# Output projection of a hybrid decoder layer: eight block products replaced by seven, for pairs of token tiles

## The reference, cut to what matters

```python
merged = g_m[:, :, 0] * (o_nsa @ w_up_nsa) + g_m[:, :, 1] * (o_dil @ w_up_dil)
mixer = merged @ w_o                                  # (1024 x 1024) @ (1024 x 1024)
x = x + g1 * mixer
h = rmsnorm(x, norm2) * (1 + sc2) + sh2
lg = h @ wg + bg;  grp = argmax(lg)                   # 4 groups of 8 experts
le = (h @ we + be) of that group;  top_v, top_i = top_k(le, 2)
x = x + g2 * (sum over the two experts of weight * (silu(h @ w1[e]) * (h @ w3[e])) @ w2[e])
out = rmsnorm(x, norm_f)
```

## Time and profile before

| | us |
|---|---|
| median of 3 runs | 1779.27 |
| lowest and highest of them | 1778.99, 1780.42 |
| the profiled execution | 1781.83 |
| its span, first to last instruction | 1780.0 |
| mean granted TensorE clock | 0.981 |

### The profile page before, as it was taken

How to read it: one execution, slowest core, us unless ns; L and a number is a source line. 1 busy time by engine, 2 the same in 40 slices (tenths; PEclk the granted TensorE clock), 3 DMA queues, 4 the chain that set the end, 5 groups by cost and what they waited for, 6 DMA issues and landing times. The chain is left out here.

```text
span 1780.0 us, 37158 instructions
## 1 busy us (share of the span) xinstructions
PE 1686.5 (95%) x16053; PEld 1128.6 (63%) x16053; DVE 607.3 (34%) x1569; ACT 415.1 (23%) x933; POOL 177.2 (10%) x219
## 2 busy tenths in 40 slices
PE   5999999999999999999999999999999999998992
PEld 3444445898777777644444445558777777777772
DVE  4533331002667666666555322261111011010103
ACT  4000000002666656510100011122212221211122
POOL 1205000000111010000000000001111111111110
PEclk9999999999999999999999999999999999999996
DMA  9874224221101107334433182149999999999985
GB/s 340 250 225 116 71 79 144 51 85 42 34 11 43 32 2 245 104 102 127 142 120 89 28 329 96 48 179 403 397 392 396 396 398 399 393 389 390 387 308 209
DMA packets 155456, 355.74 MB, mean 200 GB/s; under 512 B 15519, under 2 KB 94999, under 8 KB 138875
## 3 DMA queue, kind: packets, MB, share of 16 engines
q1 hardware_dynamic: 128112, 303.14, 45.6%
q0 software_dynamic: 13456, 27.93, 5.8%
q10 hardware_dynamic: 13724, 22.27, 3.6%
HBM read 321.58 MB, written 47.13 MB: 207 GB/s over the span
## 5 line engine op out<-in xcount | busy, mean ns | idle before, releaser
L2451 PE MATMUL psum<-sb_m_xT,sb_m_ring 128*64 128x64 f32 (+1 forms) x4096 | 174.4, 244 | 6.4 <-issue 4.2
L2451 PEld LDWEIGHTS psum<-sb_m_xT,sb_m_ring 128*64 128x64 f32 x4096 | 167.5, 138 | 19.1 <-issue 17.3
L2347 DVE TENSOR_TENSOR sb_m_hT<-psum,sb_m_sg 128x128 f32<-128x128 f32 (+1 forms) x64 | 22.1, 345 | 349.0 <-ACT sb_m_sg L2226 349.0
L2226 ACT ACTIVATE sb_m_sg<-psum 128x128 f32<-128x128 f32 (+1 forms) x64 | 20.5, 320 | 419.3 <-PE psum L2451 419.3
L2451 PE MATMUL psum<-sb_m_xT,sb_front 128*64 128x64 f32 (+1 forms) x2560 | 108.2, 242 | 9.6 <-DMA sb_m_ring<-in_exp_w_dram 4.9
L2451 PEld LDWEIGHTS psum<-sb_m_xT,sb_front 128*64 128x64 f32 x2560 | 102.7, 139 | 17.8 <-issue 16.7
L1724 PE MATMUL psum<-sb_w_o_sb,sb_mT 128*128 128x512 f32 x256 | 112.9, 595 | 0.0
L728 PE MATMUL psum<-sb_vD,sb_room 128*128 128x512 f32 x240 | 104.7, 593 | 0.2 <-DVE sb_vD L671 0.2
L2213 ACT ACTIVATE sb_m_xT<-psum,sb_rowmod 128x64 f32<-128x64 f32 (+1 forms) x256 | 84.6, 436 | 38.9 <-PE psum L2439 38.9
L988 ACT ACTIVATE sb_d_probs<-sb_d_probs,sb_d_nmax 128x640 f32<-128x640 f32 (+7 forms) x128 | 92.9, 735 | 1.5 <-DVE sb_d_nmax L1028 1.0
L760 PE MATMUL psum<-sb_b_wvd,sb_rows 128*128 128x256 f32 x384 | 88.9, 394 | 0.0
(11 more groups left out here) (346 smaller groups left out, 2418.5 us busy)
## 6 DMA issues: line engine op xcount, KB each, us to landing
sb_m_ring<-in_exp_w_dram SPq DMA_DIRECT2D x48, 2048.0 KB, 30.2
sb_front<-in_exp_w_dram SPq DMA_DIRECT2D x30, 2048.0 KB, 31.6
sb_rows<-in_exp_w_dram SPq DMA_DIRECT2D x18, 2048.0 KB, 31.1
sb_g_ada<-in_ada_w_dram SPq DMA_DIRECT2D x16, 1024.0 KB, 5.2
d_qk<-sb_n_b_sel ACTq DMA_DIRECT2D x20, 512.0 KB, 3.0
sb_front<-in_w_in_dram SPq DMA_DIRECT2D x16, 512.0 KB, 5.2
sb_front<-d_qk SPq DMA_DIRECT2D x15, 512.0 KB, 6.9
sb_n_b_sel<-in_w_in_dram SPq DMA_DIRECT2D x10, 512.0 KB, 8.9
```

What stands on the lines that cost most here:

```text
L2451: mm = pe.matmul(k.psum[part, c // 2, col:col + w], views[which][:, kk, c * P + CAPS * h:c * P + CAPS * (h + 1)], x[:, kk, 0:w], start=(kk ...
```

## The change

The 1024 x 1024 product `merged @ w_o` is cut into 2 x 2 blocks: tokens in tile `u` and tile `u + 4`, input channels in two halves, output channels in two halves. For each pair of tiles `u` (four of them), seven products M1 to M7 of four matmuls each take the place of 32 matmuls. They are computed from sums of blocks:

- sums of the weight blocks, once: `t1 = b12 - b11`, `t2 = b22 - t1` on VectorE, and `b12 <- b22 - b12`, `t4 = t2 - b21` on GpSimd, each 128 x 2048;
- sums of the activations, four of 128 x 512 for each pair, on VectorE (`row_sums`, `row_sum3`, `row_sum4`);
- sums of the products, on VectorE: each of the four result blocks takes one more addition (in `residual`), and three partial sums (`add`: u2, u5, u3); ScalarE copies M1 out of PSUM (`m1`).

The seven products go through four PSUM banks in turn. Tiles are routed in the order `TILE = [4, 0, 5, 1, 6, 2, 7, 3]`, in pairs behind the products of the next pair. `choose` runs for the first four positions while the last pair is computed, and for the other four at the end (`FIRST = NT - 4`), and the last product M3 stands behind the count of the first four. The weight sums `t1`, `t2` live in slot 2 of `front`, so the first expert's third matrix is fetched only after the last product and behind the last store. One of the three idle products at the end of the first stage is taken away, and one is added (four for three) before the last count.

```diff
+TILE = [4, 0, 5, 1, 6, 2, 7, 3]
...
-            idle_products(pe, k, 4, 3)
+            idle_products(pe, k, 4, 2)
...
+        t1, t2 = wide(2 * 4 * D), wide(2 * 4 * D + HK * BANK)
+        t4 = sb("t4", [P, HK, BANK])[:, :, :]
+        bank = lambda u, i: (7 * u + i) % 4
...
-        FIRST = NT - 2
+        FIRST = NT - 4
...
-            for i, w in enumerate((k.exp_w1, k.exp_w3, k.exp_w2)):
+            for i, w in enumerate((k.exp_w1, k.exp_w3)):
...
+            sp.wait_ge(s_done, done(NPAIR - 1, M3))
+            sp.dma_start(*expert_matrix(k.exp_w2, slice(0, 1), k.front[:, 4 * D * 2:4 * D * 3], True)).then_inc(k.s_first[2], 16)
...
+            for u in range(NPAIR):
+                a11, a12, a21, a22 = quarters(u)
+                product(u, M1, a11, b11)
+                if u == 0:
                     pe.wait_ge(s_last, 1)
+                else:
+                    turn(2 * u - 2, 0)
+                    turn(2 * u - 2, 1)
+                product(u, M2, a12, b21)
+                if u >= 1:
...
+                    route(2 * u - 2)
+                    turn(2 * u - 1, 0)
+                    turn(2 * u - 1, 1)
+                pe.wait_ge(s_sums, 4 * u + 2)
+                pe.wait_ge(s_wide, 2)
+                product(u, M6, s2, t2)
+                if u >= 1:
+                    route(2 * u - 1)
+                product(u, M5, s1, t1)
...
+                pe.wait_ge(s_wide2, 1)
+                product(u, M7, a21, b12)
+                pe.wait_ge(s_wide2, 2)
+                product(u, M4, a22, t4)
+                if u == NPAIR - 1:
+                    pe.wait_ge(s_hot, 1)
...
+                    for t in range(FIRST):
+                        mm = later(t, False)
+                    mm.then_inc(s_rank, 1)
+                pe.wait_ge(s_sums, 4 * u + 4)
+                product(u, M3, a12, b22)
+            turn(NT - 2, 0)
+            turn(NT - 2, 1)
             turn(NT - 1, 0)
+            route(NT - 2)
             turn(NT - 1, 1)
             route(NT - 1)
-            pe.wait_ge(s_mul, 2 * NT - 2)
-            idle_products(pe, k, 1, 3)
+            pe.wait_ge(s_used, used(NPAIR - 1, C12))
+            idle_products(pe, k, 1, 4)
...
+            dve.wait_ge(s_wo, 32)
+            tt(t1, b12, b11, ALU.subtract).then_inc(s_wide, 1)
+            dve.wait_ge(s_wide, 1)
+            tt(t2, b22, t1, ALU.subtract).then_inc(s_wide, 1)
+            row_sums(0)
...
+        @block.gpsimd
+        def _(pool):
+            pool.wait_ge(s_wo, 32)
+            pool.wait_ge(s_wide, 1)
+            pool.tensor_tensor(b12, b22, b12, ALU.subtract).then_inc(s_wide2, 1)
+            pool.wait_ge(s_wide, 2)
+            pool.tensor_tensor(t4, t2, b21, ALU.subtract).then_inc(s_wide2, 1)
```

More of the change, by code:

```diff
@@ L1685, in stage_out @@
         s_sum, s_sum0 = k.sem("h_sum"), k.sem("h_sum_first")
+        s_done, s_used, s_m1, s_sums, s_wide, s_wide2 = (k.sem("h_" + n) for n in (
+            "products", "products_used", "m1_out", "row_sums", "column_sums", "column_sums_pool"))
         s_x2 = [k.sem(f"h_residual{i}") for i in range(4)]
@@ L1721, in _, with product @@
         def _(pe):
[L1722 to L1727, removed]
+            def product(u, i, x, w):
+                n = 7 * u + i
+                if n >= 4:
+                    was, j = divmod(n - 4, 7)
+                    pe.wait_ge(s_m1 if j == M1 else s_used, was + 1 if j == M1 else used(was, last_use[j]))
+                for kk in range(HK):
+                    mm = pe.matmul(k.psum[:, bank(u, i), :], x[:, kk, :], w[:, kk, :], start=(kk == 0), stop=(kk == HK - 1))
+                mm.then_inc(s_done, 1)
             ones, tri = k.const[:, K_ONE:K_ONE + P], k.const[:, K_TRI:K_TRI + P]
@@ L1772, in _ @@
                     mm.then_inc(s_shift, 1)
[L1773 to L1790 removed]
+                pe.wait_ge(s_sums, 4 * u + 3)
+                pe.wait_ge(s_wide2, 1)
[4 more added lines that the diff above has]
+                    pe.wait_ge(s_hot, 1)
+                    pe.wait_ge(s_modT, 2)
+                    pe.matmul(k.psum[:, 7, 0:(NT + 1) * NE], tri, both.rearrange("p t e -> p (t e)"), start=True, stop=False)
+                    for t in range(FIRST):
[5 more added lines that the diff above has]
+            turn(NT - 2, 1)
+            turn(NT - 1, 0)
+            route(NT - 2)
             turn(NT - 1, 1)
[L1792 to L1794 removed]
             route(NT - 1)
[L1796 to L1797 removed]
+            pe.wait_ge(s_used, used(NPAIR - 1, C12))
+            idle_products(pe, k, 1, 4)
             pe.wait_ge(s_hot, 2)
@@ L1892, in _ @@
             v.inc(dve.memset(both[:, FIRST:, :], 0.0)); v.wait(dve)
-            for t in range(NT):
-                if t == NT - 1:
-                    dve.wait_ge(s_sum0, 16)
-                    dve.wait_ge(s_xn, 1)
-                    choose(0, FIRST)
-                residual(t, 0)
-                if t >= 1:
-                    turned(t - 1)
-                    if t == 1:
+            row_sum3(0)
+            for u in range(NPAIR + 1):
+                if u >= 1:
+                    root(2 * u - 2)
+                    if u == 1:
                         dve.wait_ge(s_shift, 1)
```

202 lines of the change are left out of this document (131 added, 71 removed).

## The result

The changed kernel takes **1795.15 us** (median of 4 runs, 1793.21 to 1796.25) beside 1779.57 us for the kernel before (4 runs on the same chip): a ratio of **1.0086**, 95% interval 1.0069 to 1.0103. It is slower, as forecast, but by 15.6 us instead of 8.9, and 1.2 us above the upper end of the range.

What follows compares the result with a forecast made beforehand. TensorE was taken to be busy nearly everywhere, with DMA full too in the expert stage, which starts from be_i. Terms -2.8 + 8.6 + 2.4 + 1.9 - 1.2 = +8.9 us on 1779.27 gave 1788.2 us, range 1781.5 to 1794.

Steps and rivals of the forecast that it cites:

- Fewer products, two tiles at the end, choice and counts (-2.8): In the w_o product stage: 16 fewer matmuls against a longer stage end, without contention or clock loss; -2.8 us.
- Turns at SBUF (+8.6): Ahead of the first M6: s1 and s2 on VectorE each wait for a whole GpSimd subtraction, stalling TensorE; +8.6 us.
- The first rival: At the weight sums: s1 goes first, so only one GpSimd instruction is in the way; 4.3 instead of 8.6, chance 0.14.
- the second (sums hidden): At the weight sums: GpSimd and VectorE don't collide on 2048 columns; -4.0 us, 1775.3 or 1777.2, chance 0.13.
- The clock behind that wait (+2.4): In the first M6 and after: TensorE's clock is low following its long wait for s2; +2.4 us.
- The clock at the end (+1.9): At the stage's end: the open 4.0 us wait ahead of the count lowers TensorE's clock; +1.9 us, between 0 and +7.
- a rival with a chance of 0.08: Behind the last product: the tail stays at low clock; up to +5 us more, 1790 to 1795, chance 0.08.
- One idle product less (-1.2): End of the first stage: one idle product fewer lets everything behind go on earlier; -1.2 us, between -1.8 and +0.4.
- The later fetch of the third matrix (0): Behind the last xn store: the moved 2 MB fetch arrives before TensorE needs it; 0, at most +3 us.
- `be_i` moves the end (x1): At the start of the expert stage: whatever moves the be_i cast moves the kernel's end by the same amount.

Runs made afterwards that it cites:

- sums_vector: The changed kernel with both GpSimd subtractions (b12 and t4) issued on VectorE behind s1 and s2; 1782.45 us, ratio 1.0012 to the kernel before.
- idle_tail: The changed kernel with nine idle products where TensorE waits at the end of the stage, order unchanged; 1786.38 us, ratio 1.0039 to the kernel before.
- one_gpsimd: The changed kernel with b12 left early on GpSimd and only t4 moved to VectorE behind s2; ratio 1.0060 to the kernel before.
- idle_front: The changed kernel with ten idle products on TensorE in the wait ahead of the first M6; ratio 1.0073 to the kernel before.
- count_behind: The changed kernel with the first count and its wait for the choice moved behind the last product M3; 1785.65 us, ratio 1.0035 to the kernel before.
- two_repairs: The changed kernel with b12 and t4 on VectorE behind s2 and the first count behind M3; ratio 0.9984 to the kernel before.
- best: The changed kernel with b12 and t4 on VectorE, first count behind M3 and four idle products in the tail; ratio 0.9956 to the kernel before.
- sums_late: The changed kernel with both subtractions left on GpSimd but waiting until s2 is through; 1784.91 us, ratio 1.0027 to the kernel before.

## Why the prediction was wrong

The direction and the main mechanism, the turns, were right. The mechanism of the low clock at the end was named, but its term was mis-sized, and that is where the sum failed. By its own steps, against the stage's +13.1:

- **Fewer products, two tiles at the end, choice and counts (-2.8).** Right: sums_vector has no contention, 145.3; less the 6.0 that idle_tail gives back, that would be 139.3, or -3.3 against 142.6 (worked out from two runs, not measured in one). The open wait ahead of the count was 3.59 (forecast 4.0), the stretch from last product to last route 9.9 at full clock (10.2).
- **Turns at SBUF (+8.6).** Right: 8.47. The order `t2`, `b12`, `s1`, `t4`, `s2` came as worked through, and GpSimd's 2048 columns took 4.35 us of their own, where I had 4.5. The first rival (`s1` slips in) is what one_gpsimd builds by hand, and the second (sums hidden) what sums_vector builds; neither happened by itself.
- **The clock behind that wait (+2.4).** 1.93, shown twice (sums_vector, idle_front); between 1.5 and 2.1 over the four traces with the wait of 9.21.
- **The clock at the end (+1.9). This is the step that failed: it measured 6.0.** I priced it as one fall, from one wait, that slows the count, and had the rest of the tail at full clock. The count with M3 did cost 1.7 of the 6.0. The other 4.3 came behind M3, where TensorE waits 2.55 and 1.73 us between pieces of work of 1 to 5 us, and where I had written down "waits of 2.9 and 2.2 us" myself, as the case for a rival with a chance of 0.08. It is a second fall, not the rest of the first: M3 takes 3.83 us, nearly its 3.60 at the full clock, and the turn behind it 1.04. count_behind and two_repairs show that it needs no long wait ahead of it, but comes later without one and costs 2.8 us (two_repairs against best); the other 1.5 or so went together with the count's wait. The numbers were in my text; what was missing was to ask, for each sparse stretch that the change makes, at which clock it runs. Before, this stretch had no such gaps, so the trace of before didn't show the fall, but it showed one after a single wait of 4.89 us, with the work behind it at half speed.
- **One idle product less (-1.2).** In the first pair of traces the stretch behind the first idle product is 1.7 shorter, and the stage of the change begins 0.6 earlier. The clock there differs between runs by more (5.5 against 7.7 us, and up to 2.3 us in the next stage), so that what one product less is worth can't be told from whole runs.
- **The later fetch of the third matrix (0).** Right: it goes out 10 us ahead of the `be_i` cast and is there when it is needed:

```profile
1186.01 1.18 SPq L1736 DMA_DIRECT2D sb_front<-in_exp_w_dram  x1
...
1230.84 7.03 PE L2581 MATMUL psum<-sb_front,sb_m_hT 128*128 128x512 f32 x16
```

  In these rows of the changed kernel, of SyncE and TensorE, the matrix's first products start without an idle time ahead.
- **`be_i` moves the end (x1).** Right within 0.6 us in the first pair, up to 1 us on the average above. Together with the medians, whose difference is 2.5 us more than that of the profiled spans, it carried the result past the upper end; with the clock term right, the forecast would have been 1792.3.

## What to carry to other kernels

When a change moves a small elementwise instruction beside a large one of GpSimd, price it at the large one's length, and look at who is queued behind it: the same two GpSimd instructions delayed TensorE by 8.5 us when started ahead of `s1` and `s2`, and by 1.5 us when started behind them. When a change makes a stretch of TensorE sparse, work out its time at half clock first, and fill the waits with products into a free bank: nine of them gave 6 us here, and four made the difference between a repair that can just be told and a kernel 0.44% faster than before. Before judging a saving of a few microseconds, find a pair of instructions around the changed stage, as the ratios of whole runs, with 2 to 3.5 us to either side, were too coarse to tell the steps apart; and look in several traces how far that stretch varies by itself, which was up to 1 us here.

## What was not expected of the hardware

- Behind the same wait of 3.59 us the same count and product took 7.1 us in four traces and 8.1 in two: the low clock doesn't end at the same place in every run.
- The clock fell a second time in the tail although it had been back at 1.00 from 1170 to 1176 us (window of the changed kernel), with single waits of only 2.55 and 1.73 us there.
- The clock in the first stage, at 44 to 49 us, was 0.50 in some traces and 1.00 in others of the same code up to there, which alone makes 2.1 us (7.7 against 5.5).
- The size of the instruction that waits hardly mattered: a 128 x 288 multiplication and a 128 x 512 subtraction took 4.76 and 4.70 us beside GpSimd instructions of some 4.36 of their own (sums_late).
